# A chunk scan on one core of a Trainium2: head sums split into 64-column pieces, and the order of TensorE's small products

## The reference, cut to what matters

```python
def step(s, inp):
    r_t, w_t, k_t, v_t, aa_t, bb_t = inp
    sa = jnp.einsum('bhij,bhj->bhi', s, aa_t)
    s = s * w_t[:, :, None, :] + sa[..., None] * bb_t[:, :, None, :] + v_t[..., None] * k_t[:, :, None, :]
    return s, jnp.einsum('bhij,bhj->bhi', s, r_t)
...
kk = kk / jnp.maximum(jnp.sqrt(jnp.sum(kk * kk, axis=-1, keepdims=True)), 1e-12)
...
mean = jnp.mean(y, axis=-1, keepdims=True)
var = jnp.mean(jnp.square(y - mean), axis=-1, keepdims=True)
bonus = (jnp.sum(r_h * k_h * r_k.astype(f32), axis=-1, keepdims=True) * v_h).reshape(bsz, t, c)
```

## Time and profile before

| what | value |
| --- | --- |
| time, median of 3 (lowest, highest) | 3142.97 us (3138.88, 3146.47) |
| span of the profiled execution | 3144.1 us (no other time of that execution is shown) |
| TensorE busy: matmuls, weight loads | 3010.5 us, 2891.6 us |
| VectorE, ScalarE, GpSimd busy | 1805.6, 1023.8, 965.1 us |
| the chunk scan | about 1650 to 2141 us of the span |

### The profile page before, as it was taken

One profiled execution on the slowest core, in us unless ns is written; L12 is line 12 of the kernel. 1 busy time (PEld: TensorE's weight loads), 2 busy tenths in 40 slices (PEclk: granted clock), 3 DMA queues, 4 the chain that ended last, 5 costly groups with the idle time before them and its releaser, 6 DMA issues.

```text
span 3144.1 us, 66739 instructions
## 1 busy us (share of the span) xinstructions
PE 3010.5 (96%) x29234; PEld 2891.6 (92%) x29234; DVE 1805.6 (57%) x1884; ACT 1023.8 (33%) x1281; POOL 965.1 (31%) x549
## 2 busy tenths in 40 slices
PE   8999999999999997889998999998999999999998
PEld 7899999999999997889997777887999999999997
DVE  7766765555656557512206777773566555565657
ACT  6533411111111113633326667764311111111113
POOL 1322223222222223313314555552132322222221
PEclk9999999999999999999998999999999999999999
DMA  3111111111111111242232222213111111111111
GB/s 107 46 44 41 39 44 41 48 48 41 48 41 48 41 48 34 81 174 86 90 110 73 70 69 71 75 48 102 41 48 41 41 48 48 41 48 41 48 41 71
DMA packets 88684, 185.66 MB, mean 59 GB/s; under 512 B 29024, under 2 KB 53088, under 8 KB 88416
## 3 DMA queue, kind: packets, MB, share of 16 engines
q1 hardware_dynamic: 81504, 154.73, 15.6%
q10 hardware_dynamic: 6912, 26.84, 2.1%
HBM read 145.01 MB, written 36.53 MB: 58 GB/s over the span
## 4 chain that ended last, share of the span: by engine, by line
PE 78%; DVE 14%; ACT 5%; issue 1%; POOL 1%; DMA 1%; DVEq 0%; SPq 0%; ACTq 0%; POOLq 0%
PE PS L1306 64%; PE PS L1516 10%; DVE T L1764 3%; DVE X L1764 2%; DVE T L1779 2%; PE PS L1442 2%; ACT T L512 2%; DVE BK L1764 1%; DVE HL L1774 1%; ACT L512 1%; DVE G L1764 1%; PE PS L1396 1%; DVE T L1774 1%; ACT UV L512 1%; PE PS L1358 1%
## 5 line engine op out<-in xcount | busy, mean ns | idle before, releaser
L1089 POOL TENSOR_TENSOR WL<-RAW,WH 128x1024 fp32r<-128x1024 f32 x204 | 496.0, 2432 | 1393.4 <-ACT WH L512 1389.5
L1306 PE MATMUL PS<-HH,WH 128*128 128x364 f32 x3456 | 771.8, 331 | 31.9 <-DVE HL L1774 12.7
L1306 PE MATMUL PS<-HH,WL 128*128 128x364 f32 x3456 | 767.4, 330 | 0.0
L1306 PE MATMUL PS<-HL,WH 128*128 128x364 f32 x3456 | 764.3, 330 | 0.0
L1306 PEld LDWEIGHTS PS<-HH,WH 128*128 128x128 f32 x3456 | 601.1, 189 | 41.5 <-issue 15.8
L1306 PEld LDWEIGHTS PS<-HH,WL 128*128 128x128 f32 x3456 | 605.7, 189 | 0.0
L1306 PEld LDWEIGHTS PS<-HL,WH 128*128 128x128 f32 x3456 | 603.0, 189 | 0.0
L512 ACT ACTIVATE WH<-RAW 128x1024 fp32r<-128x1024 f32 x204 | 216.7, 1062 | 825.9 <-PE PS L1306 809.6
L1764 DVE TENSOR_TENSOR T<-PS,T 128x1092 f32<-128x1092 f32 x110 | 142.6, 1296 | 552.4 <-PE PS L1306 535.6
L1764 DVE TENSOR_TENSOR X<-PS,X 128x1092 f32<-128x1092 f32 (+2 forms) x240 | 292.8, 1220 | 235.1 <-PE PS L1306 216.6
L1306 PE MATMUL PS<-PH,WH 128*128 128x364 f32 x1248 | 278.2, 331 | 10.2 <-DVE X L1764 5.2
(11 more groups left out here) (191 smaller groups left out, 3458.8 us busy)
## 6 DMA issues: line engine op xcount, KB each, us to landing
RAW<-weights SPq DMA_DIRECT2D x204, 512.0 KB, 3.3
scratch<-T ACTq DMA_DIRECT2D x31, 546.0 KB, 3.1
scratch<-SR ACTq DMA_DIRECT2D x14, 546.0 KB, 2.9
X<-xT SPq DMA_DIRECT2D x8, 546.0 KB, 7.7
T<-scratch_m SPq DMA_DIRECT2D x8, 512.0 KB, 3.7
KK<-scratch SPq DMA_DIRECT2D x16, 192.0 KB, 2.9
LW<-scratch SPq DMA_DIRECT2D x16, 192.0 KB, 2.8
AA<-scratch SPq DMA_DIRECT2D x16, 192.0 KB, 3.2
```

What stands on the lines that cost most here:

```text
L1089: pool.tensor_tensor(out, full, hi, ALU.subtract).then_inc(*t.made(event))
L1306: mm = pe.matmul(acc[:, j, :], a, b[:, j * CW:(j + 1) * CW], start=(i == 0 and q == 0), stop=(i == len(blocks) - 1 and q == 2))
```

## The change

Only TensorE's instructions change. A head sum is made of one product for each chunk and head, 64 columns wide (`sum_of`), where it was one product for each head; the means and variances are issued so in their old places. The key squares move from before link(0) into left(3), and the bonus sums from behind link(4) into left(4): for each chunk the left product, then the sum's piece. The spread products move from beside the lower products to beside left(5), and the lower products follow alone. At level 2 the left product now comes before the move of the same chunk. The two halves of a link are separate functions, issued one after the other as before. The waits that stood at the head of each group stand at the head of the combined group.

```diff
@@ -1520,39 +1520,56 @@
                 def tile(bank, h, i, w=CHUNK):
                     return PS[HALF[h], bank, i * w:(i + 1) * w]
 
-                def sums(src, event, reader, count):
+                def sums_bank(reader, count):
 
                     nonlocal bank2
                     if bank2:
                         pe.wait_ge(*t.at(*bank2))
                     bank2 = (reader, count)
+
+                def sum_of(src, at, i, n, event):
+
                     for h in range(HEADS):
-                        mul(PS[HALF[h], 2, 0:src.shape[-1]], CO[HALF[h], C_BD + h * CHUNK:C_BD + (h + 1) * CHUNK],
-                            src[HALF[h]], event)
-
-                def key_squares():
+                        mul(tile(2, h, i), CO[HALF[h], C_BD + h * CHUNK:C_BD + (h + 1) * CHUNK],
+                            src[HALF[h], (at + i) * CHUNK:(at + i + 1) * CHUNK], event if i == n - 1 else None)
+
+                def key_squares_begin():
 
                     if has_k and job > -3:
                         held(("k_sq", job + 4))
-                        sums(X2[:, ka * CHUNK:kz * CHUNK], "s_kk", "k_max", job + 4)
+                        sums_bank("k_max", job + 4)
+
+                def key_square_of(i):
+
+                    if has_k and job > -3 and ka + i < kz:
+                        sum_of(X2, ka, i, kz - ka, "s_kk")
 
                 def means():
 
                     if has_n:
                         held(("k_ys", job))
-                        sums(flat(Y)[:, na * CHUNK:nz * CHUNK], "s_mean", "k_cent", job)
+                        sums_bank("k_cent", job)
+                        for i in range(nz - na):
+                            sum_of(flat(Y), na, i, nz - na, "s_mean")
...
-
-                def bonus_sums():
+                        sums_bank("k_gln", job)
+                        for i in range(nz - na):
+                            sum_of(Q1, na, i, nz - na, "s_var")
+
+                def bonus_sums_begin():
 
                     if has_p:
                         held(("k_prep", q + 1))
-                        sums(X3[:, pa * CHUNK:pz * CHUNK], "s_bon", "k_bonus", q + 1)
+                        sums_bank("k_bonus", q + 1)
+
+                def bonus_of(i):
+
+                    if has_p and pa + i < pz:
+                        sum_of(X3, pa, i, pz - pa, "s_bon")
...
-                def moves_and_left(k):
+                def moves_begin():
 
                     if has_s:
                         held(("k_we", job + 1), ("k_sae", 2 * job + 2))
+
+                def move(i):
+
+                    if has_s and a + i < z:
+                        for h in range(HEADS):
+                            mul(PAIR[HALF[h], i * P:(i + 1) * P], W[HALF[h], i, :], G[HALF[h], a + i, h, CHUNK:],
+                                "k_rp" if a + i == z - 1 else None)
+
+                def left_begin(k):
+
                     if has_l:
                         held(("k_mc", mc * inv + k - 1))
+
+                def left(i):
+
+                    if has_l and la + i < lz:
+                        for h in range(HEADS):
+                            mul(tile(6, 1 - h, i), G[HALF[h], la + i, h, 0:CHUNK], M[HALF[h], i, :],
+                                "k_lm" if la + i == lz - 1 else None)
+
+                def left_and_moves():
+
+                    left_begin(2)
+                    moves_begin()
                     for i in range(6):
-                        if has_s and a + i < z:
-                            for h in range(HEADS):
-                                mul(PAIR[HALF[h], i * P:(i + 1) * P], W[HALF[h], i, :], G[HALF[h], a + i, h, CHUNK:],
-                                    "k_rp" if a + i == z - 1 else None)
-                        if has_l and la + i < lz:
-                            for h in range(HEADS):
-                                mul(tile(6, 1 - h, i), G[HALF[h], la + i, h, 0:CHUNK], M[HALF[h], i, :],
-                                    "k_lm" if la + i == lz - 1 else None)
+                        left(i)
+                        move(i)
...
-                def link(i):
+                def source(c):
+                    return SIN if c == NCH - 1 else SS[(c - 1) % 2]
...
+                def link_state(i):
 
                     c = a + i
                     if not has_s or c >= z or c == 0:
                         return
-                    S = SIN if c == NCH - 1 else SS[(c - 1) % 2]
-                    held(("k_s", NCH * f + c), *([("dma_sin", f + 1)] if c == NCH - 1 else []),
-                         *([("k_pp", job + 1)] if i == 0 else []))
+                    link_ready(c)
+                    if i == 0:
+                        held(("k_pp", job + 1))
                     for h in range(HEADS):
-                        mul(tile(0, h, i), PT[HALF[h], i, :], S[HALF[h], :], "k_ch", False)
+                        mul(tile(0, h, i), PT[HALF[h], i, :], source(c)[HALF[h], :], "k_ch", False)
...
-
-                def left_times(k):
-
-                    if not has_l:
-                        return
-                    held(("k_mc", mc * inv + k - 1))
-                    for i in range(la, lz):
-                        for h in range(HEADS):
-                            mul(tile(6, 1 - h, i - la), G[HALF[h], i, h, 0:CHUNK], M[HALF[h], i - la, :],
-                                "k_lm" if i == lz - 1 else None)
...
-                def lower_and_spread():
+                def lower_begin():
 
                     if has_p:
                         held(("k_bkt", q + 1), ("k_eye", 1))
+
+                def lower(i):
+
+                    if has_p and pa + i < pz:
+                        for h in range(HEADS):
+                            mul(PAIR[HALF[1 - h], i * P:(i + 1) * P], AR[HALF[h], pa + i, 0, :],
+                                BK[HALF[h], pa + i, 2 * h::3 - 2 * h, :], "k_l0" if pa + i == pz - 1 else None)
+
+                def spread_begin():
+
                     if has_l:
                         held(("k_mc", mc * (inv + 1)), ("k_vt", 2 * inv + 2))
+
+                def spread(i):
+
+                    if has_l and la + i < lz:
+                        for h in range(HEADS):
+                            mul(tile(7, 1 - h, i), G[HALF[1 - h], la + i, h, 0:CHUNK], UV[HALF[1 - h], la + i, h, :],
+                                "k_ra" if la + i == lz - 1 else None)
+
+                def left_and_key_squares():
+
+                    left_begin(3)
+                    key_squares_begin()
                     for i in range(6):
-                        if has_p and pa + i < pz:
-                            for h in range(HEADS):
-                                mul(PAIR[HALF[1 - h], i * P:(i + 1) * P], AR[HALF[h], pa + i, 0, :],
-                                    BK[HALF[h], pa + i, 2 * h::3 - 2 * h, :], "k_l0" if pa + i == pz - 1 else None)
-                        if has_l and la + i < lz:
-                            for h in range(HEADS):
-                                mul(tile(7, 1 - h, i), G[HALF[1 - h], la + i, h, 0:CHUNK], UV[HALF[1 - h], la + i, h, :],
-                                    "k_ra" if la + i == lz - 1 else None)
+                        left(i)
+                        key_square_of(i)
+
+                def left_and_bonus_sums():
+
+                    left_begin(4)
+                    bonus_sums_begin()
+                    for i in range(6):
+                        left(i)
+                        bonus_of(i)
+
+                def left_and_spread():
+
+                    left_begin(5)
+                    spread_begin()
+                    for i in range(6):
+                        left(i)
+                        spread(i)
+
+                def lower_alone():
+
+                    lower_begin()
+                    for i in range(6):
+                        lower(i)
 
...
                 fresh_state()
-                moves_and_left(2)
+                left_and_moves()
                 fresh_out()
                 grow(2)
-                key_squares()
-                link(0)
-                left_times(3)
-                link(1)
+                link_state(0)
+                link_out(0)
+                left_and_key_squares()
+                link_state(1)
+                link_out(1)
                 value_turn()
-                link(2)
+                link_state(2)
+                link_out(2)
                 grow(3)
-                link(3)
+                link_state(3)
+                link_out(3)
                 products(0)
-                left_times(4)
-                link(4)
-                bonus_sums()
+                left_and_bonus_sums()
+                link_state(4)
+                link_out(4)
                 products(1)
-                link(5)
+                link_state(5)
+                link_out(5)
                 grow(4)
                 key_turn()
-                left_times(5)
-                lower_and_spread()
+                left_and_spread()
```

(33 more changed lines are left out.)

## The result

The changed kernel takes 3176.38 us (median of 4, 3173.47 to 3179.13), the kernel before 3144.57 us beside it (median of 4): a ratio of 1.0104, 95% interval 1.0092 to 1.0117, so 32 us more where 24 were forecast. The profiled execution took 3179.13 us.

The account below looks back on a forecast made before the run. It took the scan as bound by a chain of VectorE results and partly by late 256-instruction fetches. Fetches 13.5 + 7 and chain 3.2 made plus 24 us on 3142.97: 3167 us, 8-in-10 range 3144 to 3196.

Parts of the forecast that it names:

- Folded sums gain nothing: Key squares in left(3), bonus sums in left(4): about 1.2 us freed per interval, lost waiting for M and G; gain 0.
- Link(1) 0.2 us later: Behind left(3), link(1) must follow the last key-square piece, delaying VectorE's mask of B: plus 0.2 us an interval.
- Left(4) 0.07 us later: The weighted-keys wait, moved ahead of left(4), delays it and link(4)'s state: plus 0.07 us, bounds 0 and 0.2.
- Means and variances in pieces, 0 to 0.05 each: Chunk-wise sums in their old places: at most 0.05 us more each; taken as 0, bound 0.1 an interval.
- Spread, lower, left before move: 0: Spread beside left(5), lower products alone, left product before move at level 2: no change in time, 0.
- 14 more fetches: Over the scan, the added instructions bring 14 more packets on the instruction queue.
- Early intervals: The scan's nine early intervals, paced by instruction fetches: 21.5 us each, plus 1.5 each, 13.5 us in all.
- The later intervals: The scan's twelve later intervals: halts rise from 0.5 to 1.3 us, plus 0.6 each, 7 us in all.
- the chain's 3.2: Late link(1) and left(4) in the twelve later intervals: (0.2 + 0.07) x 12 = 3.2 us; hidden in early ones.
- Hidden fetches: Rival: fetches across the scan stay hidden, only the chain's delays cost, 6.2 us: 3149 us; chance 0.20.
- the gain: Rival: the folded sums' time comes back at left(3) and products(1), up to 28 us: 3115 to 3129 us; chance 0.15.
- Fetches everywhere: Rival: fetches bind in all 22 intervals at 4.30 us each, up to 66 us more: 3190 to 3209 us; chance 0.10.

Follow-up runs that it names:

- e6: Changed kernel with means and variances whole, key squares and bonus sums in two pieces of up to 192 columns: 3147.13 us, 1.0022 to the kernel before.
- e8: e6 with the state half of link(1) issued inside left(3), ahead of its fourth chunk: 3152.71 us, 1.0037 to the kernel before.
- e9: Kernel before with the state half of link(1) issued inside left(3), ahead of its fourth chunk: 3142.11 us, 0.9997.
- e4: Changed kernel with means and variances whole again, key squares and bonus sums still in pieces inside the left products: 3154.25 us, 1.0034 to the kernel before.
- e3: Kernel before with only means and variances in pieces, in their old places: 3154.25 us, 1.0035.
- e1: Changed kernel's order with every head sum whole and in its old place: 3144.17 us, 1.0006 to the kernel before.
- e2: Kernel before with all four head sums in pieces, in their old places: 3174.67 us, 1.0101.
- e7: Kernel before with 32 one-column products, 128 instructions, once ahead of the scan, shifting every 256-instruction border half a block: 3146.78 us, 1.0021.
- e5: Kernel before with ten (eight for five chunks) one-column products ahead of each whole bank of sums, 448 more instructions in three intervals: 3213.45 us, 1.0225.

## Why the prediction was right, and where it was off

- **Folded sums gain nothing.** Right. Left(3) waits for M in 20 of 21 intervals, with 0.47 us of idle array in front in the median (about 0.6 forecast), and e6 shows the freed time turned into waits for M and G. Products(1) waits for G less often than forecast (11 waits after), because left(4) and link(4) now reach past G's end.
- **Link(1) 0.2 us later.** Its first matmul came 0.23 us later (0.82 against 0.58 us after the end of M, medians), but the mask behind it only 0.09 us. VectorE's other work was not what hid the rest, for it stood idle ahead of the link's state for longer than before (0.62 against 0.35 us, medians). The link itself was quicker: its four state records start within 0.07 us where they took 0.11, and from the first of them to VectorE's state it is 0.40 us instead of 0.55. e8 and e9 show that this mask doesn't set the pace alone. The term was too large, and the step "this is on the chain" holds only in part.
- **Left(4) 0.07 us later.** Too small in some intervals. The mask behind left(4) starts 0.11 us after G in the median of the kernel after, as before, but in 8 of 21 intervals by more than 0.3 us (before in 1); in e4 the median is 0.63, in e6 with its wide pieces 0.11. That the bonus pieces hold link(4) back is my reading. It costs nothing visible: e4 has the largest lag and costs what e3 does.
- **Means and variances in pieces, 0 to 0.05 each.** The step holds: 0.70 us for six chunks against 0.65.
- **Spread, lower, left before move: 0.** Right (e1).
- **14 more fetches.** Right to the packet: 231 to 245. **Early intervals** were put at 21.5 us, from 4.1 us a fetch; they take 21.20.
- **The later intervals** are where the size was off. I took them as led by the chain of results, since their halts were short (3.4 us over seven), and let each grow by 0.6 us. They grew by 2.1, to the length of the early ones. So twelve of them brought 25 us where 7 and the chain's 3.2 were forecast, and the nine early ones 10.6 us where 13.5 were. The measured 3176 lies inside the range, but part of that is luck: the early term and the chain were put too high, the late term far too low. In place of that step the runs show one pace of about 4.0 us for 256 instructions over the whole scan, which the later intervals before, at 4.10 us a fetch, had all but reached: a short halt did not mean room. By my own rate of 4.1 used throughout, (21.5 - 19.58) x 21 = 40 us; measured 32 to 33.
- **A count.** The text puts the 256 instructions of the earlier trace rows together from some 252 records and the separate waits. By their starts each of those three windows holds 256 loads and matmuls without a wait; 3614 has no waits in it either, so the sums stand.
- **The rivals.** Hidden fetches are refuted by e2, the gain by e6. Fetches everywhere had the right extent, but 4.30 us for each was too high a rate: it came from three halts chosen because they were visible.

The Trainium skill ("Runtime: NRT & Kernel Launch", Instruction fetch mechanics) calls the cost of a crossing mostly hidden. In this scan that is not so: e2 adds 14 fetches and 32 us.

What stays open: why the crossings of before were dear early and cheap later. In e7, with the borders moved, and in e9, with them where they were, the early intervals are no longer the slow ones, so it is no fixed property of the early stretch, and the place of the borders alone doesn't make it either. Each kernel has one profile, so no run shows how much the halts of one kernel differ from execution to execution. Of the 32 us, the part of the new order can't be told from zero (1.0104 after, 1.0101 in e2, each with some 0.15% either way).

## What to carry to other kernels

Count instructions as well as array time: split four-instruction fp32 products only where the stretch has room above its cost per 256 instructions. Divide an interval by its fetches; if several kernels or stretches give the same quotient (here 4.0 us), that is the pace, and short halts are no sign of slack. Work that fills a wait for another engine gives nothing back when it is made free; first see what ends the wait, and whether a second result ends with it.

## What the runs showed of the hardware

- A dense run of TensorE instructions was held to 3.96 to 4.07 us for 256 instructions in four kernels with added pieces, halts of up to 2.0 us included. Where one-column products kept TensorE busier (e5) it was 4.21 us.
- A one-column fp32 product of 64 rows by 64 weight columns took 57 ns a record when all lay in one quarter (e5). A left product puts 12 records of 64 columns into each of two quarters in 0.70 us, 58 ns each: fewer columns saved next to nothing.
- 64 one-column records (32 products, 128 instructions) ahead of the scan put its first product 3.9 us later, and with it the end of the scan; moving the borders of 256 by half a block changed the halts from 11.9 to 11.7 us (e7).
- Every 256th load or matmul of TensorE, waits not counted, is where the halts stand, and 3544 more of them came with 14 more packets on the instruction queue.
